# Hyena's token projection as seven products, and the rows of V subtracted once in stick-breaking attention

## The reference, cut to what matters

```python
def stick_breaking_attention(q, k, v):          # block by block of 128 queries
    z = q @ k.T * scale
    strict = pos_k < pos_q
    log_keep = where(strict, log_sigmoid(-z), 0)
    log_rest = reverse_cumsum(log_keep) - log_keep
    a = where(strict, exp(log_sigmoid(z) + log_rest), 0)
    return a @ v

def hyena_mixer(h, w_in, b_in, short_w, short_b, ...):
    u = centred_depthwise_conv(h @ w_in + b_in, short_w, short_b)   # 3 taps along the tokens
    v, x1, x2 = split(u, 3)                                         # 3072 columns
    z = x1 * two_sided_fft_conv(v, filter 0)
    z = x2 * two_sided_fft_conv(z, filter 1)
    return z @ w_out + b_out
```

## Time and profile before

| | |
|---|---|
| median of 3 runs | 3180.3 us (3179.01 to 3183.41) |
| profiled execution, from its first to its last instruction | 3177.3 us |
| mean granted clock of PE | 0.978 of full speed |
| HBM read | 592.73 MB, 190 GB/s over the span |
| DVE, ACT, POOL busy | 47%, 23%, 11% of the span |

### The profile page before, as it was taken

One profiled execution on the slowest core, in us unless ns is written; L12 is line 12 of the kernel. 1 busy time (PEld: TensorE's weight loads), 2 busy tenths in 40 slices (PEclk: granted clock), 3 DMA queues, 4 the chain that ended last, 5 costly groups with the idle time before them and its releaser, 6 DMA issues.

```text
span 3177.3 us, 36092 instructions
## 1 busy us (share of the span) xinstructions
PE 3005.1 (95%) x14479; PEld 1659.0 (52%) x14479; DVE 1491.1 (47%) x2829; ACT 724.1 (23%) x1521; POOL 355.3 (11%) x218
## 2 busy tenths in 40 slices
PE   8999899998989899999999999999989887999998
PEld 5888443787744344446856533333345543444443
DVE  5994842998392434675575311211144753011112
ACT  1210542121262201111124201100015642111111
POOL 4553000655200000000001100000000000000000
PEclk9999999999999899999999899999999998999999
DMA  5452003456201222110412799999931003999997
GB/s 225 164 194 80 27 1 129 155 184 244 80 1 40 108 83 106 36 53 8 169 67 88 314 389 399 376 389 377 396 122 56 24 3 148 412 421 421 421 421 295
DMA packets 89896, 606.07 MB, mean 191 GB/s; under 512 B 10809, under 2 KB 11612, under 8 KB 19205
## 3 DMA queue, kind: packets, MB, share of 16 engines
q1 hardware_dynamic: 79776, 575.70, 45.4%
q0 software_dynamic: 4432, 15.73, 1.6%
q10 hardware_dynamic: 5524, 12.35, 1.2%
HBM read 592.73 MB, written 11.01 MB: 190 GB/s over the span
## 4 chain that ended last, share of the span: by engine, by line
PE 63%; DVE 7%; ACT 2%; issue 1%; another core or an unknown queue 0%; DVEq 0%; ACTq 0%; PEldq 0%
PE ps L1359 8%; PE ps L2763 7%; PE ps L2725 7%; PE ps L2776 4%; PE ps L2742 4%; PE ps L2806 4%; PE ps L1092 3%; PE ps L3056 2%; PE ps L2613 2%; PE ps L1457 2%; PE ps L2815 2%; PE ps L2529 2%; PE ps L2630 2%; PE ps L1697 2%; PE ps L3217 1%; PE ps L1509 1%
## 5 line engine op out<-in xcount | busy, mean ns | idle before, releaser
L611 PE MATMUL ps<-mem 128*128 128x256 f32 x1792 | 393.3, 381 | 13.2 <-DVE mem L641 10.8
L611 PEld LDWEIGHTS ps<-mem 128*128 128x128 f32 x1792 | 340.3, 191 | 65.5 <-DVE mem L641 14.4
L556 POOL TENSOR_TENSOR mem<-mem 128x512 f32<-128x512 f32 (+1 forms) x160 | 301.7, 1885 | 535.2 <-DVE mem L852 276.5
L754 DVE SCALAR_TENSOR_TENSOR mem<-mem 128x1024 f32<-128x1024 f32 x160 | 254.7, 1632 | 13.8 <-DMA mem<-in_ada_w 12.9
L1359 PE MATMUL ps<-mem 128*128 128x512 f32 (+1 forms) x768 | 254.7, 494 | 2.9 <-ACT mem L1200 2.9
L2763 PE MATMUL ps<-mem 128*64 128x512 f32 x1024 | 223.3, 594 | 0.0
L2725 PE MATMUL ps<-mem 128*64 128x512 f32 x1024 | 222.5, 592 | 0.7 <-ACT mem L2659 0.7
L1359 PEld LDWEIGHTS ps<-mem 128*128 128x128 f32 x768 | 147.5, 193 | 109.5 <-issue 98.3
L641 DVE TENSOR_TENSOR mem<-ps,mem 128x256 f32<-128x256 f32 x308 | 121.3, 418 | 111.9 <-PE ps L611 68.4
L1092 PE MATMUL ps<-mem 128*128 128x512 f32 x384 | 169.6, 597 | 1.8 <-DVEq L156 1.8
L2915 DVE TENSOR_TENSOR mem<-ps,mem 128x512 f32<-128x512 f32 x16 | 11.1, 691 | 314.1 <-PE ps L2725 314.1
(11 more groups left out here) (420 smaller groups left out, 4156.9 us busy)
## 6 DMA issues: line engine op xcount, KB each, us to landing
mem<-in_moe_w SPq DMA_DIRECT2D x384, 1024.0 KB, 13.9
mem<-in_w_in SPq DMA_DIRECT2D x48, 1024.0 KB, 8.1
mem<-in_ada_w SPq DMA_DIRECT2D x48, 1024.0 KB, 5.0
mem<-in_hy_w_in SPq DMA_DIRECT2D x24, 1024.0 KB, 6.9
mem<-in_w_out SPq DMA_DIRECT2D x12, 1024.0 KB, 6.0
mem<-in_k_win_l SPq DMA_DIRECT2D x8, 1024.0 KB, 6.9
mem<-in_hy_w_out SPq DMA_DIRECT2D x8, 1024.0 KB, 5.0
mem<-in_sw_w_in SPq DMA_DIRECT2D x6, 1024.0 KB, 7.1
```

The lines of the kernel that those rows point to most:

```text
L556: gp(out, x, y, op).then_inc(A.mark(sem), 1)
L611: m = mm(seven(l, unit), x[:, k, :], y[:, k, :], start=(k == 0), stop=(k == 3))
L754: stt(PRODUCT if again else w, w, 1.0, C_ROWS[:, z, :], ALU.mult, ALU.mult, accum_out=mod(layer, b // KD, b % KD, z))\
```

## The change

In attention the difference is moved from the weights to the rows of V. With K the cumulative product, the weight of key j is K(j+1) - K(j), and the sum over j of weight times V(j) equals the sum of (K(j) - 1) times (V(j-1) - V(j)). At the start of the phase ACT issues two DMAs that copy the stick-breaking rows of V shifted by one key (1 MB and a row), POOL subtracts them in four operations, ACT's evacuation adds -1 while it copies, and DVE's subtraction and the columns of ones go. `pe_pv` of the first stick-breaking head waits for POOL.

The token projection gets functions of its own. Tiles 0 to 3 stay plain; the other 20 are ten pairs of seven products in four banks. POOL makes the sums. ACT makes the centre tap with all biases folded into one column; DVE makes the two outer taps, a pair later, between the additions of a pair, and the filter work is cut into six pieces that go there too. The edges of a tile hold minus the bias. `end_phase(together=False)` reports the arrival and goes on without waiting for the others. The two spectrum buffers of the tokens change places, since the tile buffers now live on into the next phase. Five semaphores are shared with names that other phases use.

```diff
-def end_phase(A):
+def end_phase(A, together=True):
...
-    A.e.wait_ge(A.sems["arrived"], 3 * A.sems.phase)
+    if together:
+        A.e.wait_ge(A.sems["arrived"], 3 * A.sems.phase)
...
+        def act_move_rows(A):
+            own = VN[:, NQ:2 * NQ, :]
+            A.e.dma_start(V_BEFORE[1:P], own[0:P - 1]).then_inc(S["v_moved"], 16)
+            A.e.dma_start(V_BEFORE[0:1, 1:NQ, :], own[P - 1:P, 0:NQ - 1, :]).then_inc(S["v_moved"], 16)
+
+        def pool_attn(A):
+            A.last, A.counts = None, {}
+            nc.gpsimd.memset(V_BEFORE[0:1, 0, :], 0.0).then_inc(A.mark(), 1)
+            A.e.wait_ge(*A.last)
+            A.e.wait_ge(S["v_moved"], 32)
+            for i in range(NQ):
+                own = VN[:, NQ + i, :]
+                nc.gpsimd.tensor_tensor(own, V_BEFORE[:, i, :], own, ALU.subtract).then_inc(A.mark("v_stepped"), 1)
...
+            if (kind, pair) == (1, 0):
+                A.e.wait_ge(S["v_stepped"], NQ)
...
-                    act(dst, src, ACT.Copy).then_inc(A.mark("turned_out"), 1)
+                    if kind == 1:
+                        act(dst, src, ACT.Identity, bias=MISC[:, 3:4]).then_inc(A.mark("turned_out"), 1)
+                    else:
+                        act(dst, src, ACT.Copy).then_inc(A.mark("turned_out"), 1)
...
-                        A.e.wait_ge(*A.last)
-                        tt(pset[:, :, 512 - kw:512], pset[:, :, 513 - kw:513], pset[:, :, 512 - kw:512], ALU.subtract)\
-                            .then_inc(A.mark("weights"), 1)
...
+        def t_bank(j, i):
+            return T_USE[j, i] % 4
...
+        def pool_hy_tokens(A):
+            A.e.wait_ge(S["h_ready"], KD)
+            made(T_RIGHT[0], right(0, 1), right(0, 0), ALU.subtract, "data_folded")
+            made(T_RIGHT[1], right(1, 1), T_RIGHT[0], ALU.subtract, "data_folded")
+            made(T_RIGHT[2], right(1, 1), right(0, 1), ALU.subtract, "data_folded")
+            made(T_RIGHT[3], right(1, 0), T_RIGHT[1], ALU.subtract, "data_folded")
+            for j in T_PAIRS:
...
+                SUMS = ((w(1, 0), w(1, 1), ALU.add, 2), (x[0], w(0, 0), ALU.subtract, 1),
+                        (w(0, 0), w(1, 0), ALU.subtract, 3), (w(0, 1), x[1], ALU.subtract, 5))
...
+        def pe_token_pair(A, j):
+            PRODUCTS = ((w(0, 0), right(0, 0), 0), (x[1], T_RIGHT[1], 2), (x[0], T_RIGHT[0], 0), (x[2], T_RIGHT[2], 3),
+                        (w(0, 1), right(1, 0), 0), (x[3], right(1, 1), 4), (w(1, 1), T_RIGHT[3], 0))
+            for i, (one, two, sums) in enumerate(PRODUCTS):
+                A.e.wait_ge(*t_bank_taken(j, i))
+                if sums:
+                    A.e.wait_ge(S["sums_made"], 4 * t_pair(j) + sums)
...
+                for k in range(4):
+                    m = mm(t_out(j, i), one[:, k, :], two[:, k, :], start=(k == 0), stop=(k == 3))
...
+        def pe_hy_tokens(A, st):
+            for j in T_PAIRS:
+                pe_token_pair(A, j)
+                for t in range(TOK.ne):
+                    if j + 1 == FILTER_AT[t]:
+                        pe_token_filter(A, t)
...
+            A.e.wait_ge(S["filter_folded"], TOK.ne)
+            A.e.wait_ge(S["product_read"], t_read(22, 6))
+            end_phase(A, together=False)
...
+        def act_token_centre(A, j, src):
+            act(TOK.U3[:, j, :], src, ACT.Identity, bias=T_ADD[:, j:j + 1], scale=gv("hy_sw", 24 + j))\
+                .then_inc(A.mark("centre_made"), 1)
...
+        def dve_token_conv(A, j):
+            nc.vector.tensor_copy(u[:, ::T + 1], T_EDGE[:, j:j + 1].to_broadcast([P, 2])).then_inc(A.mark(), 1)
+            A.e.wait_ge(*A.last)
+            A.e.wait_ge(S["centre_made"], j + 1)
+            stt(o, u[:, 0:T], gv("hy_sw", j), o, ALU.mult, ALU.add).then_inc(A.mark(), 1)
+            A.e.wait_ge(*A.last)
+            stt(o, u[:, 2:T + 2], gv("hy_sw", 48 + j), o, ALU.mult, ALU.add).then_inc(A.mark("dve_out"), 1)
+
+        def dve_token_pair(A, j, between):
+            A.e.wait_ge(S["copied"], t_pair(j) + 1)
+            A.e.wait_ge(S["dve_out"], j - 2)
+            add(C[1][0], 1, C[0][0])
+            between(0)
+            add(C[0][1], 2, C[1][0])
+            add(C[1][1], 3, C[0][1], None)
+            add(C[1][0], 3, C[1][0])
+            between(1)
+            add(C[0][0], 4, C[0][0])
+            add(C[0][1], 5, C[0][1])
+            add(C[1][0], 6, C[1][0])
...
+            for j in T_PAIRS:
+                def between(n, j=j):
+                    dve_token_conv(A, j - 2 + n)
+                    step = 2 * t_pair(j) + n - 2 * t_pair(FILTER_AT[0] + 1)
+                    if step in (0, 3):
+                        dve_filter(A, TOK, 0, step // 3, 4 * (step // 3), 4)
+                    elif step > 0:
+                        dve_filter_fold(A, TOK, step // 3, step % 3 - 1)
+                dve_token_pair(A, j, between)
+            dve_token_conv(A, 22)
+            dve_token_conv(A, 23)
+            end_phase(A, together=False)
```

More of the change, by code:

```diff
@@ L206, in build @@
                 sems[n] = ctx.enter_context(nc.semaphore(f"{n}_{turn}"))
-            nums = [x.num for x in sems.values()]
+            for n, other in SHARED_SEMS.items():
+                sems[n] = sems[other]
+            nums = sorted({x.num for x in sems.values()})
             assert max(nums) - min(nums) == len(nums) - 1
@@ L1246, in __init__ @@
                 other = (HT_, HT_ + 2048)[n]
[L1247 removed]
+                s.KS = [v(at, 4 * s.ne, 512) for at in ((other, KS_), (KS_, other))[n]]
                 s.Q_ = (HT_ + KD * T, HT_)[n]
@@ L1314, in dve_filter_fold, with hy_constants, act_hy_sines @@
                 tt(rb, x1, rb, ALU.subtract).then_inc(A.mark("filter_folded"), 1)
+        def hy_constants(y):
+            return [(v(FWD_, 4 * y.ne * y.H), a[f"k_fwd_{y.tag}"]), (v(INV_, 4 * y.ne * (y.H + 1)), a[f"k_inv_{y.tag}"]),
+                    (y.ALT, a[f"k_alt_{y.tag}"]),
+                    (v(HR_, y.L, p=33), a[f"k_pos_{y.tag}"]), (v(FB_, 64, p=33), a["hy_ffn_w1_2"]),
+                    (v(FB_ + 64, P, p=64), a["hy_ffn_w2_2"])]
+        def act_hy_sines(A, y):
+            for r in range(2):
+                A.e.wait_ge(S["b_ready"], r + 1)
+                act(v(H2_, y.L, p=(64, P)[r]), v(y.Q_, y.L, p=(64, P)[r]), ACT.Sin).then_inc(A.mark("c_ready"), 1)
         def act_hy_a(A, y):
@@ L1318, in act_hy_a @@
             L = y.L
[L1319 to L1326, removed]
+            act_mod_norm(A, y.n, v(KS_, KD, L), v(y.Q_, L), 0, 0, 1, loads=hy_constants(y))
+            act_hy_sines(A, y)
             for j in range(24):
@@ new lines, in pool_hy_tokens, with made @@
+        def pool_hy_tokens(A):
+            gp = nc.gpsimd.tensor_tensor
+            def made(out, x, y, op, sem):
+                if A.last:
+                    A.e.wait_ge(*A.last)
+                gp(out, x, y, op).then_inc(A.mark(sem), 1)
+            A.last, A.counts = None, {}
+            A.e.wait_ge(S["h_ready"], KD)
[3 more added lines that the diff above has]
+            made(T_RIGHT[3], right(1, 0), T_RIGHT[1], ALU.subtract, "data_folded")
+            free = [0] * len(T_LEFT)
+            for j in T_PAIRS:
+                n, t = DEPTH * N_HYB + j // 4 * 2, j % 4
+                for half in range(2):
+                    A.e.wait_ge(S[f"w_in{PLACE[n + half]}"], LANDED[n + half])
+                w = lambda i, k: quarter(t_slot(j), t, i, k)
+                x = [T_LEFT[t_left(j, i)] for i in range(4)]
+                SUMS = ((w(1, 0), w(1, 1), ALU.add, 2), (x[0], w(0, 0), ALU.subtract, 1),
+                        (w(0, 0), w(1, 0), ALU.subtract, 3), (w(0, 1), x[1], ALU.subtract, 5))
+                for i, (one, two, op, product) in enumerate(SUMS):
+                    if free[t_left(j, i)]:
+                        A.e.wait_ge(S["product"], free[t_left(j, i)])
+                    made(x[i], one, two, op, "sums_made")
+                    free[t_left(j, i)] = t_product(j, product)
@@ new lines, in dve_hy_tokens @@
+        def dve_hy_tokens(A):
+            dve_mod_norm(A, 0, None, v(TOK.Q_, T), 0, 0, "norm1", 1, TOK.norm_banks, summed=True)
+            tt(T_ADD, gv("hy_sw", 0, 24), gv("hy_sw", 24, 24), ALU.add).then_inc(A.mark(), 1)
+            ts(T_EDGE, gv("hy_b_in", 0, 24), -1.0, None, ALU.mult).then_inc(A.mark(), 1)
+            A.e.wait_ge(*A.last)
+            tt(T_ADD, T_ADD, gv("hy_sw", 48, 24), ALU.add).then_inc(A.mark(), 1)
+            A.e.wait_ge(*A.last)
+            tt(T_ADD, T_ADD, gv("hy_b_in", 0, 24), ALU.mult).then_inc(A.mark(), 1)
+            A.e.wait_ge(*A.last)
+            tt(T_ADD, T_ADD, gv("hy_sb", 0, 24), ALU.add).then_inc(A.mark("shift_ready"), 1)
+            dve_hy_angles(A, TOK)
+            for j in range(T_PLAIN - 2):
+                dve_token_conv(A, j)
+            for j in T_PAIRS:
+                def between(n, j=j):
[8 more added lines that the diff above has]
+            dve_token_conv(A, 23)
+            end_phase(A, together=False)
```

149 lines of the change are left out of this document (125 added, 24 removed).

## The result

The changed kernel took 3219.9 us (median of 4 runs, 3218.6 to 3222.6), the kernel before in the same session 3179.7 (3178.6 to 3183.4): ratio 1.0127, 95% interval 1.0114 to 1.0139. It is 40 us slower where 16 us faster was forecast. Its profiled execution spans 3217.9 us against 3177.3, so the 40.6 us can be looked for stage by stage.

What follows compares the result with a forecast made beforehand. TensorE, busy 95% of the span, was taken to bound the kernel, with VectorE setting the pace in the attention heads. Terms -16.5 + 3.8 + 0.3 - 0.3 - 7.0 + 1.0 + 2.3 = -16.4 us gave 3164 us, range 3153 to 3176.

Steps and rivals of the forecast that it cites:

- The rows of V: Start of attention: ACT's two DMA issues hidden, at most +0.5 us a layer; 1 MB lands in 6.0 us.
- Rival E: Attention: V rows come late, PE waits in the fifth head and the 7.0 us are lost; 3171 us, chance 0.03.
- The products: Token projection: ten pairs of seven products replace twenty tiles, 137.4 to 120.9 us, -16.5 us.
- The stalls in the late pairs: Token projection: PE waits for DVE, slowed beside POOL, in the last three pairs; +3.8 us, bounds 0 and 9.9.
- The open end: Between token projection and spectrum: PE idles 2.8 us instead of 3.11, -0.3 us, slow clock behind it unchanged.
- the start of the sines: Start of token projection: sine arguments slowed beside POOL's first sums, +0.3 us, bounds 0 and 1.
- The stick heads: Stick-breaking heads: DVE's subtraction over the weights goes, -7.0 us over both layers; ACT's Identity with bias costs +1.0.
- Contention in the differential heads: Differential heads: DVE slowed beside POOL's four subtractions, 0.3 us in layer 0 and 2.0 in layer 1; +2.3, bounds 0 and 8.3.
- Nothing behind it takes it back: Rest of the kernel: later stages keep the gain, since the weight stream waits on slots and phases that move with it.
- D: Rival, stick-breaking heads: Identity after Sigmoid makes ScalarE reload its function table in every block; 3213 us, chance 0.04.
- B: Rival: POOL and DVE hardly meet and the clock holds over the open end; 3155 to 3158 us, chance 0.20.
- C: Rival, late pairs and attention: DVE waits out every POOL sum; stalls of 9.3 and 8.3 us, 3175 us, chance 0.18.

Runs made afterwards that it cites:

- e1: Changed kernel with the 127-row copy of V issued as two copies, of 112 and 15 rows: 3180.1 us, 1.0001 of the kernel before.
- e2: Changed kernel with the one-row copy issued first and the 127-row copy second: 3177.2 us.
- e7: Attention of the kernel before with the changed token projection, POOL's data sums waiting for the first sine angle: 3168.9 us, 0.9955 to 0.9980 of before.
- e12: Plain copies for Identity, on the changed kernel with split, later-issued copies, V rows subtracted by DVE, POOL's sums after the first sine angle: 3160.3 us against 3158.6.
- e6: Changed kernel with the copy split in 112 and 15 rows and V rows subtracted by DVE at the stick heads' start, not by POOL: 3166.1 us.

## Why the prediction was wrong, step by step

**The step that failed** is "The rows of V": the issues of ACT were called "hidden, at most +0.5 a layer", on the price of a pair of issues elsewhere (1.16 us), and the copy was given the 6.0 us of a weight load. Both rows show transfers of another shape. The copy has 127 rows; it ran at 27 GB/s, landed after 46 us and held the issue behind it by 19.55 and 20.86 us. PE's wait at this place grew by 39.5 us over both layers. That is the loss: the differential heads lost 47.6 us in all, and the 8 of them beyond this wait are nearly balanced by the 7.1 that the stick heads gained. e1 takes the 40 us back. The Trainium skill, DMA: Bandwidth & Descriptors, section "Why a DMA increments its semaphore by 16 and not by 1", says that a copy is spread over the largest number of engines up to 16 that divides its row counts, and names 127 partitions as a case of one. The trace agrees, with 6.3% of 16 engines and 27 GB/s for 127 rows, and 10.95 us of waiting for 112 and 15. Rival E had the rows late, by 40 us even, but looked for the price in the fifth head; e2 shows that this alone costs 2 us in layer 0 and 4 in layer 1.

**Other terms.** The products: forecast -16.5; seven pairs at 12.14 us make 121.4 for ten, -16.0. The stalls in the late pairs: 2.57 for 3.8. The open end: a gap of 3.02 us, where 2.8 was forecast and 3.11 stood before. The three make -13.5, and e7, where nothing else disturbs, has -13.8. (Behind the gap the spectrum took 15.68 us at a granted clock of 0.89, for 16.83 at 0.84, so part of the clock came back.) What the forecast missed here is the start of the sines, 0.3 us with 1 as the bound: it was 3.42 us of wait, and behind it 16.33 us, at a granted clock of 0.85, for 32 records that take 14.00 in e7, 5.8 in all. I had looked at two-input operations only; the six angle steps, 3.4 us undisturbed, took 9.6 beside POOL's sums, single-input ones among them (0.42 to 2.45). The Trainium skill, SBUF - State Buffer, section "Who interferes with whom", allows for that: tensor_scalar can enter a mode with two ports and then contends with GpSimd.

The stick heads: the subtraction's end brought 3.6 us a layer net, 7.1 in all, where -7.0 + 1.0 stood; with Identity's 1.8 (e12) the gross gain is 8.9. So the gain exceeded the bound that was read from PE's waits for that line alone. Contention in the differential heads, forecast 2.3: two waits of 1.91 and 1.63 us in the changed kernel, and in e1 5.1 and 2.7 us more to the values of head 4 than in e6, which has the same three issues and no POOL there. That is 7.8 us, three times the forecast, though within its bound of 8.3. "Nothing behind it takes it back" failed as well, by 5.3 us in the projections of layer 1.

**Rivals.** D forecast 3213 us and came nearest by number, but not by cause: ACT's table loads in the two attentions are the six of before, and none stands at the evacuations. The late pairs lie between B (no stall) and C (9.3 us), as the forecast had them.

## What to carry to other kernels

Before pricing a DMA by another one of the same bytes, compare their row counts: a copy shifted by one partition has 127, and splitting it in 112 and 15 took it from 45 to 11 us. Price the instruction behind an issue too, since rows still waiting in the queue can hold the engine that issues next, 20 us here, and put short transfers ahead of long ones. Work moved to GpSimd was paid here by VectorE, whose operations on SBUF took two to six times as long beside it, so it belongs where VectorE has no one waiting, or on VectorE itself.

## What was not expected of the hardware

A second issue on a queue waits for the first one's rows and not for its bytes alone: 127 rows of 8 KB held it for 20 us, 127 of 2 KB for 7, 61 of 8 KB not at all. And one memset of 0.5 us on GpSimd, some 255 us ahead of a stage, changed the order in which GpSimd and VectorE took turns there, by 2.6 us of TensorE's time.
